# Rebuilding the matrix recurrence of a two-block network: division, evictions and Fourier products in pieces, mask on GpSimd

## What is computed

```python
    def step(carry, xs):
        ...
        w_intra = jnp.exp(D - m_t[..., None])
        s = jnp.einsum('bhtd,bhsd->bhts', qc, kc) * w_intra
        numer = jnp.einsum('bhts,bhsd->bhtd', s, vc) + w_state[..., None] * ...
        denom = jnp.sum(s, axis=-1) + w_state * ...
        h = numer / jnp.maximum(jnp.abs(denom), jnp.exp(-m_t))[..., None]
...
h_fwd = mlstm_chunkwise(q, k, v, i_pre[0], f_pre[0])
h_bwd = flip(mlstm_chunkwise(flip(q), flip(k), ...))
h = (h_fwd + h_bwd).transpose(0, 2, 1, 3)
...
y = jnp.fft.fftn(zg, axes=(1, 3), norm='ortho').real     # fnet_mixer
return jnp.einsum('bsgc,gce->bsge', y, w) + b
```

## Time and profile before

| what | us |
|---|---|
| median of 3 runs | 3979.68 |
| lowest and highest run | 3979.65, 3983.33 |
| the profiled execution | 3976.05 |
| its span in the trace | 3974.3 |

### The profile page before, as it was taken

One profiled execution on the slowest core, in us unless ns is written; L12 is line 12 of the kernel. 1 busy time (PEld: TensorE's weight loads), 2 busy tenths in 40 slices (PEclk: granted clock), 3 DMA queues, 4 the chain that ended last, 5 costly groups with the idle time before them and its releaser, 6 DMA issues. The chain is left out here.

```text
span 3974.3 us, 42227 instructions
## 1 busy us (share of the span) xinstructions
PE 3742.9 (94%) x16750; PEld 2885.9 (73%) x16750; DVE 2247.2 (57%) x3076; ACT 1276.4 (32%) x1827; POOL 659.3 (17%) x346
## 2 busy tenths in 40 slices
PE   8999997999999999987999979898999999989999
PEld 6888733788878888534888856686788777867887
DVE  6545555754564445457655575775544567755443
ACT  3222233522242223334422244334222343343221
POOL 3441000244214430000443102020000020200000
PEclk9999997999999999997999989898999998989999
DMA  4343200344323342101434212001222220012222
GB/s 167 137 138 105 89 23 5 131 135 135 119 96 124 133 139 86 57 23 56 140 136 139 94 62 71 17 1 54 80 97 98 85 77 24 1 39 86 98 97 80
DMA packets 92949, 345.44 MB, mean 87 GB/s; under 512 B 10833, under 2 KB 11089, under 8 KB 91857
## 3 DMA queue, kind: packets, MB, share of 16 engines
q1 hardware_dynamic: 92752, 342.74, 25.9%
HBM read 340.60 MB, written 2.10 MB: 86 GB/s over the span
## 5 line engine op out<-in xcount | busy, mean ns | idle before, releaser
L381 ACT ACTIVATE w_hi<-raw 128x1024 fp32r<-128x1024 f32 (+2 forms) x540 | 561.1, 1040 | 1919.7 <-PE ps L325 1906.0
L323 PE MATMUL ps<-xs_hi,w_hi 128*128 128x512 f32 x2472 | 980.1, 396 | 34.9 <-DVE xs_lo L538 14.5
L324 PE MATMUL ps<-xs_lo,w_hi 128*128 128x512 f32 x2472 | 970.0, 392 | 0.0
L325 PE MATMUL ps<-xs_hi,w_lo 128*128 128x512 f32 x2472 | 969.4, 392 | 0.0
L391 DVE TENSOR_TENSOR w_lo<-raw,w_hi 128x1024 fp32r<-128x1024 f32 (+2 forms) x540 | 669.0, 1240 | 128.5 <-ACT w_hi L381 128.3
L323 PEld LDWEIGHTS ps<-xs_hi,w_hi 128*128 128x128 f32 x2472 | 468.2, 189 | 158.9 <-issue 32.7
L776 POOL TENSOR_SCALAR arena<-arena,parg 128x768 f32<-128x768 f32 x128 | 304.5, 2390 | 1656.3 <-PE ps L325 910.1
L325 PEld LDWEIGHTS ps<-xs_hi,w_lo 128*128 128x128 f32 x2472 | 468.7, 190 | 99.1
L324 PEld LDWEIGHTS ps<-xs_lo,w_hi 128*128 128x128 f32 x2472 | 469.0, 190 | 98.1 <-issue 3.4
L323 PE MATMUL ps<-hd_hi,w_hi 128*128 128x512 f32 x1320 | 527.9, 400 | 4.6 <-DVE hd_lo L483 3.5
L324 PE MATMUL ps<-hd_lo,w_hi 128*128 128x512 f32 x1320 | 525.1, 398 | 0.0
(11 more groups left out here) (425 smaller groups left out, 4202.9 us busy)
## 6 DMA issues: line engine op xcount, KB each, us to landing
raw<-in_ffn_gu SPq DMA_DIRECT2D x264, 512.0 KB, 3.7
arena<-in_ada SPq DMA_DIRECT2D x64, 768.0 KB, 5.6
raw<-in_ffn_dn SPq DMA_DIRECT2D x96, 448.0 KB, 3.3
raw<-in_in_t SPq DMA_DIRECT2D x60, 512.0 KB, 3.6
raw<-in_ffn_dn SPq DMA_DIRECT2D x48, 512.0 KB, 3.5
raw<-in_out SPq DMA_DIRECT2D x32, 512.0 KB, 3.6
raw<-in_pleg SPq DMA_DIRECT2D x16, 512.0 KB, 3.6
raw<-in_in_r SPq DMA_DIRECT2D x8, 512.0 KB, 3.9
```

The lines of the kernel that those rows point to most:

```text
L323: T.matmul(bank, lhs_hi(k), rhs_hi(k), start=(first and k == 0), stop=False)
L324: T.matmul(bank, lhs_hi(k), rhs_lo(k), start=False, stop=False)
L325: mm = T.matmul(bank, lhs_lo(k), rhs_hi(k), start=False, stop=(last and k == kt - 1))
L381: A.activation(self.hi[:, n % HL, 0:size], raw[:, n % RAW, 0:size], ACT.Copy).then_inc(self.high_done, 1)
```

## The change

It rewrites the instruction lists of this one stage. In short:

- **Accumulators.** `sums(q, e)`: directions 0, 1 and 3 use banks 5 and 6; direction 2 uses banks 0 and 1, where the scores had been, once all sixteen are copied. `num` and `den` exist twice; the second pair lies in a part of the buffer of the Fourier stage (`second`). At the first step of directions 1 and 3 PE waits for the eviction of the same bank by an earlier direction (e + 1 or e + 3 of `evacuated`).
- **Eviction** by e: two copies after the third exponential of the direction's second group for e = 0, two after the second exponential of the next direction for e = 1.
- **Division.** `bound` (two DVE instructions) after the second weighting of the next direction, then `invert`, a quarter of the reciprocal, behind each of the next four weightings. Multiplication and addition are POOL's for directions 0 to 2. The last division is whole, on DVE, at the end.
- **Mask** on POOL for all 32 steps, behind a new semaphore `weighted`; POOL had no work in this stage before.
- **Fourier products** one by one: one at the first and one at the second step of a group, ahead of the step's product, two at the third. So the first of them stands ahead of step 0, with its wait for the loads.
- **Spreads** of M and of the threshold, and the scores, move: the first two spreads before the scores; four scores before the steps, two pairs at steps 0 and 1, and one pair at the fourth step of each of groups 0 to 3; the spread of M at a group's second step; the spread of the threshold at the fourth step of each e = 0 group.
- DVE waits for the scores one by one (`qk_copied`) instead of eight at a time.

```diff
+        dens, nums = [sp_.get(S), second[:, 0, :]], [sp_.get(S), second[:, 1, :]]
+        NP = 4
+        PIECE = S // 4
+        sums = lambda q, e: ps[e if q == 2 else 5 + e]
...
-            def fourier(pe, j):
+            def fourier(pe, j, k):
                 bank = ps[4][:, :]
-                if j:
-                    pe.wait_ge(dft_copied, j)
-                else:
-                    pe.wait_ge(dft_landed, 32)
+                if k == 0:
+                    if j:
+                        pe.wait_ge(dft_copied, j)
+                    else:
+                        pe.wait_ge(dft_landed, 32)
...
             @st.block.tensor
             def _(pe):
-                for m in range(8):
+                for g in range(2):
+                    spread(pe, g)
+                for m in range(4):
                     scores(pe, m)
                 for s_, (g, j) in enumerate(steps):
...
+                    if s_ < 2:
+                        scores(pe, 4 + 2 * s_)
+                        scores(pe, 5 + 2 * s_)
+                    if k == 0:
+                        fourier(pe, g, 0)
+                    elif k == 1:
+                        if g < 6:
+                            fourier(pe, g, 1)
+                        if 1 <= g < 7:
+                            spread(pe, g + 1)
+                    elif k == 2:
+                        if g < 4:
+                            fourier(pe, g, 2)
+                            fourier(pe, g, 3)
+                    else:
+                        if g < 4:
+                            scores(pe, 8 + 2 * g)
+                            scores(pe, 9 + 2 * g)
+                        if e == 0:
+                            if q:
+                                pe.wait_ge(thr_ready, q)
+                            T.matmul(ps[7][:, :], pick_pair(36, 5 * d + p), rows_t[0:36, :], start=True, stop=True).then_inc(t_spread, 1)
+                    if k == 0:
+                        if q == 2:
+                            pe.wait_ge(qk_copied, 16)
+                        elif q:
+                            pe.wait_ge(evacuated, e + 1 if q == 1 else e + 3)
                     pe.wait_ge(wgt_ready, s_ + 1)
...
             @st.block.scalar
             def _(act):
-                for m in range(8):
+                for m in range(4):
                     scores_copy(act, m)
...
                     act.wait_ge(arg_ready, s_ + 1)
                     A.activation(...ACT.Exp).then_inc(exp_ready, 1)
+                    if s_ < 2:
+                        scores_copy(act, 4 + 2 * s_)
+                        scores_copy(act, 5 + 2 * s_)
+                    if k < 2 and 1 <= g <= 4:
+                        scores_copy(act, 6 + 2 * g + k)
+                    if k == 0 and e == 1:
+                        act.wait_ge(t_spread, q + 1)
+                        if q >= 2:
+                            act.wait_ge(dir_ready, q - 1)
+                        A.activation(thr[:, q % 2, :], ps[7][:, :], ACT.Copy).then_inc(thr_ready, 1)
+                    if k == 1 and e == 0 and q:
+                        evacuate(act, q - 1, 1)
+                    if k == 2 and e == 1:
+                        evacuate(act, q, 0)
+                    if k == 3:
                         fourier_copy(act, g)
...
+            def invert(dve, q, cols):
+                V.reciprocal(dens[q % 2][:, cols], dens[q % 2][:, cols]).then_inc(inverted, 1)
...
-                        order.done(V.tensor_tensor(wx[:, r], wx[:, r], qks[:, p, e, j, r], ALU.mult))
-                        dg = slice(j * P, (j + 1) * P)
-                        V.tensor_tensor(wx[:, dg], wx[:, dg], C("upto") if d == 0 else C("from"), ALU.mult) \
-                         .then_inc(wgt_ready, 1)
-                        if s_ > 2 * ST and s_ % (2 * ST) == 2:
-                            divide(dve, s_ // (2 * ST))
-                divide(dve, 4)
+                        V.tensor_tensor(wx[:, r], wx[:, r], qks[:, p, e, j, r], ALU.mult).then_inc(weighted, 1)
+                    q, i = divmod(s_, 2 * ST)
+                    if 1 <= q < NP and i == 2:
+                        bound(dve, order, q - 1)
+                    if 1 <= q < NP and 3 <= i <= 6:
+                        invert(dve, q - 1, slice((i - 3) * PIECE, (i - 2) * PIECE))
+                q = NP - 1
+                bound(dve, order, q)
+                invert(dve, q, slice(0, S))
...
+            @st.block.gpsimd
+            def _(pool):
+                order = Order(pool, st.sem("pool_order"))
+                for s_, (g, j) in enumerate(steps):
+                    d = groups[g][1]
+                    wx = wgt[:, s_ % 4, j * P:(j + 1) * P]
+                    pool.wait_ge(weighted, s_ + 1)
+                    G.tensor_tensor(wx, wx, C("upto") if d == 0 else C("from"), ALU.mult).then_inc(wgt_ready, 1)
+                    q, i = divmod(s_, 2 * ST)
+                    if q and i == 2 * ST - 1:
+                        q -= 1
+                        p, d = divmod(q, 2)
+                        pool.wait_ge(inverted, 4 * q + 4)
+                        if d == 0:
+                            G.tensor_tensor(hsum[:, p, :], nums[q % 2], dens[q % 2], ALU.mult).then_inc(dir_ready, 1)
+                        else:
+                            order.done(G.tensor_tensor(nums[q % 2], nums[q % 2], dens[q % 2], ALU.mult))
+                            pool.wait_ge(dir_ready, q)
+                            G.tensor_tensor(hsum[:, p, :], hsum[:, p, :], nums[q % 2], ALU.add).then_inc(dir_ready, 1)
```

More of the change, by code:

```diff
@@ L1661, in mixer1_mlstm @@
     def mixer1_mlstm(l, m, work, spectrum):
-        part, spec, dft, fw = spectrum
+        part, spec, second, dft, fw = spectrum
         y, cq, ckv, kr, mx, mo, gi, gf, vz, uq, ukv = m
@@ L1733, in scores_copy, with spread @@
                 A.activation(qks[:, m // 8, m % 2, m // 2 % ST, :], ps[m % 2][:, :], ACT.Copy).then_inc(qk_copied, 1)
+            def spread(pe, g):
+                p, d, e = groups[g]
+                if g >= 2:
+                    pe.wait_ge(arg_ready, ST * (g - 1))
+                T.matmul(ps[2 + g % 2][:, :], pick(36, 32 * d + 2 * p + e), rows_m[0:36, :], start=True, stop=True) \
+                 .then_inc(m_spread, 1)
             @st.block.tensor
             def _(pe):
-                for m in range(8):
+                for g in range(2):
+                    spread(pe, g)
+                for m in range(4):
                     scores(pe, m)
@@ new lines, in _, with bound @@
+                    if k == 3:
+                        fourier_copy(act, g)
+                evacuate(act, NP - 1, 1)
+            def bound(dve, order, q):
+                dve.wait_ge(evacuated, 2 * q + 2)
+                dve.wait_ge(thr_ready, q + 1)
+                order.done(V.scalar_tensor_tensor(out=larger, in0=dens[q % 2], scalar=-1.0, in1=thr[:, q % 2, :],
+                                                  op0=ALU.mult, op1=ALU.max))
+                V.tensor_tensor(dens[q % 2], dens[q % 2], larger, ALU.max).then_inc(bounded, 1)
+                dve.wait_ge(bounded, q + 1)
@@ L1820, in _ @@
+            def invert(dve, q, cols):
+                V.reciprocal(dens[q % 2][:, cols], dens[q % 2][:, cols]).then_inc(inverted, 1)
             @st.block.vector
             def _(dve):
-                order.eng = dve
+                order = Order(dve, st.sem("dve_order"))
                 for s_ in range(len(steps) + 1):
```

90 lines of the change are left out of this document (25 added, 65 removed).

## The result

The changed kernel took 3928.5 us (median of 4 runs, 3924.45 to 3936.29) against 3979.66 us for the kernel before, timed on the same chip (4 runs, 3979.1 to 3983.33): a ratio of 0.9872, 95% interval 0.9853 to 0.989, 51 us less. Predicted: 3934, in 3918 to 3954. The profiled execution took 3924.45 us, its span 3922.7.

What follows compares the result with a forecast made beforehand. Order and waits, no full engine, bound the two recurrence stages (107.8 and 108.1 us); head, groups and tail summed to 85 each, 46 us saved in all, so 3930 profiled and 3934 median, range 3918 to 3954.

Steps and rivals of the forecast that it cites:

- tail: End of a stage after its last product: two copies, bound, whole reciprocal, multiply and add, 7.5 us.
- Seam and division: At steps 8, 16, 24: PE no longer waits 3.50 us for eviction; reciprocal pieces of 0.95 us delay arguments at most 1.
- saved 3.5 us three times: Evicting banks early removes PE's wait for ACT's four copies at three seams: 10.5 us a stage, plus clock losses behind.
- The half clock of group 0: After PE's wait of some 3 us for the load, clock 0.50 for about 6 us, costing 3 us.
- DVE 11.9 + collisions 1.4: Groups 4 and 5, DVE bound: 11.9 us of DVE work plus 1.4 of DVE and POOL excluding each other; ends at 60.
- the lock of the earlier trace: Profile before: DVE's two-input subtraction took 2.87 us beside POOL's two-input product, 1.21 alone, waiting for POOL to end.
- Groups 6 and 7 at 17.5 us: Last two groups, 13.5 to 19 us with a POOL stall of 3 to 4 at step 24 and falling clock; 17.5 taken.
- (A): Rival: clock stays up, POOL light (mask 0.3, multiply 1.1 us), no fall at step 24; 78 us per stage, 3920; chance 0.12.
- (B): Rival: POOL masks take 0.8 to 1.1 us with lock; 92 to 95 us per stage, 3948 to 3954; chance 0.17.
- (C): Rival: slower, 1.2 GHz through the whole stage, 120 us each, 4004; slower than before beyond 23 us more half-clock work; chance 0.04.
- (D): Rival: another, unseen in-order wait holds the seams, so only 4 us go; chance 0.03.
- Another stage changed by more than 2 us: Sign that the forecast is wrong: a stage other than the two recurrence stages changes by more than 2 us.

Runs made afterwards that it cites:

- the block: The changed kernel with all Fourier products of a group in one block behind its first step, as in the kernel before: 3934.45 us, stage sum 173.8 us.

## Why the prediction was right

The sum, term by term, for the first stage (times from its start):

| term | predicted | measured |
|---|---|---|
| first Fourier product | 9.9 | 9.95, for the load |
| group 1 begins | 22.5 | 21.45 (second: 19.2) |
| group 4 begins | 47 | 47.05 |
| group 6 begins (step 24) | 60 | 62.8 |
| last product ends | 77.7 | 75.7 |
| tail | 7.5 | 7.5 |
| stage | 85 | 82.9 (second: 80.7) |
| reciprocal piece | 0.95 | 0.945 |
| mask | 0.42 | 0.46 |
| POOL busy | 19 | 19.9 |
| mean clock | 0.85 | 0.89, 0.91 |

**Seam and division** did what the sum said: no pause of PE over 0.3 us through groups 1 to 3, clock 1.00. What the sum didn't say is how the parts share it. Of the 37.4 us that the two middles lost, taking parts out one by one gives back 8.8 (pieces), 4.3 (order of the Fourier products), 4.2 (eviction) and nothing (mask), 17.3 together. The other 20 us have no part to their name: either parts cover for each other, or they belong to the moved spreads and scores and to DVE's wait for single scores, none of which any run takes back by itself. My "saved 3.5 us three times" holds for the whole change, where the three waits are gone; put in alone, the eviction leaves 2.35 us of each, and taken out of the changed kernel it costs 2.1 us a stage in the middle and not 10.5.

**The head.** The wait for the load came out to a tenth. *The half clock of group 0* was the first mis-sized term: I had 0.50 for some 6 us, it was 3 (588 to 591, then 0.94), so group 1 came 1 us early. In the second stage the load came 0.7 us sooner and the clock stayed at 1.00; group 1 began at 19.2, which is the whole difference between the two stages.

**Collisions.** "DVE 11.9 + collisions 1.4" for groups 4 and 5 was too little: group 6 came 2.8 us late, with DVE's weightings at 1.81 and 1.22 us beside POOL's long products, as the lock of the earlier trace rows has it. The run with these on DVE shows that 1.6 to 1.8 us of the delay belong to them. *Groups 6 and 7 at 17.5 us* was too much: 12.9. I took the upper part of my 13.5 to 19, mostly half clock on 9 products; the clock was back at 0.70 in 651 to 654, and the last steps of every group are narrow. Taken as lengths, with 15.8 us for groups 4 and 5 instead of 13 and 25.6 for groups 1 to 3 instead of 24.5, the errors of the first stage are -1.05, +1.1, +2.8 and -4.7, and -0.2 for a slip of mine (60 and 17.5 make 77.5, not 77.7): they nearly cancel, to -2. That cancelling was luck; the mechanism was right, these two lengths were not. With the second stage (-4.3) it is 6.4 us for both, about what the median lies under the forecast (5.5).

**The mask** at 0.46 lies by the middle value I took between 0.28 and 1.12. The Trainium skill's figure ("GPSIMD Engine Reference", section Elementwise — side-by-side cycle accounting) has about 2.6 cycles an element, by which I had estimated 0.28 us plus a dispatch that it doesn't price for such an instruction; with 1.26 us for 512 columns and 0.46 for 128 the slope is 2.1 ns a column, about the page's, and the fixed part 0.19 us.

**The rivals.** (A) asked for no fall at step 24 and 78 per stage: the run with idle products gave 79, near it, but with 15.9 us for groups 4 and 5 where (A) had 13 and 10.0 for the steps of groups 6 and 7 where it had 13, so its figure too holds by errors that cancel. (B) didn't come about; with two masks in place of one, it cost less than I had priced. (C): beside the 3 us at the head the clock was below full in the last 12 us of the steps, most of which I had counted, and it did not fall in the 23 us more that (C) needed. (D)'s mechanism is real for the eviction alone, though more than its 4 us went, and absent in the whole change. *Another stage changed by more than 2 us*, which I had named as a sign against me, did happen (the first recurrence stage starts at 578.2 instead of 580.8, with nothing changed before it); the repeat of the same kernel starts it at 580.55, so this sign was a poor one.

Still open: what the 20 us without a part belong to, and why the same pause is not always followed by the same clock. The 2.3 us at step 24 were followed by 9 us of half clock in one stage of the changed kernel, some 6 in one of its repeat and 12 with group 0's Fourier products later, and the 3.19 us of the block by 3 us in one stage and 15 in the other.

## What to carry to other kernels

When a pause at a seam goes, ask what else the first instruction behind it needs, and follow that chain through the in-order queues: here a second wait of 2.35 us stood behind one of 3.50. Long instructions on a side engine are to be cut so that they fit between two that the path needs (0.95 us pieces instead of 3.35). Short ones on POOL cost the path nothing measurable here, and no gain from them is shown; long ones in the same queue cost 1.8 us a stage before step 24. Where PE pauses for 2 to 3 us, price the half clock behind it as a range: here it lasted from nothing to 15 us. And before a small difference is read as a part's worth, look at where in the stage it arises: a stretch that repeats to 0.1 us tells what a sum that moves by 3 us can't.

## What was not expected of the hardware

- More work took less time: 7 products more per stage, 5.8 us less for two stages, with the clock at 0.98 instead of 0.90, and all of the gain behind step 24.
- The half clock did not follow the pause alone: 0.50 for 6 us with no pause over 0.94 us ahead in the stage, and 1.00 behind a pause of 2.37 us.
- The clock makes one program's stage vary by up to 4.3 us (84.75 and 89.1 us in two stages with the same instructions). The rest of the kernel varied by up to 17 us (3759.1 to 3776.6); 12 of them lie behind the second stage, where the same 9840 recorded instructions of PE took 1996.1 us in the one and 2012.2 in the other. A single profile tells a part worth 4 us only by its rows, not by its length.
- A POOL product over 128 columns costs 0.46 us and over 512 columns 1.26 us, while DVE's take 0.28 and 0.69 us; single weightings of DVE were stretched (0.69 to 1.81, 0.56 to 1.22) only beside long ones of POOL.
